# A merging stage that begins with half-products while its attention tiles are still being merged

## The reference, cut to what matters

```python
def merge_by_denominator(outs, lses):
    wts = jax.nn.softmax(jnp.stack(lses, 0), axis=0)
    return jnp.sum(wts[..., None] * jnp.stack(outs, 0), axis=0)
...
    mix = jnp.concatenate([o_dn.reshape(B, S, DN_V), o_at.astype(x.dtype).reshape(B, S, AT_W)], axis=-1) @ w_out
    x = x + rmsnorm(mix, g_post_mix)
```

## Time and profile before

| | us |
|---|---|
| median of 3 runs | 3841.65 |
| lowest, highest | 3839.93, 3842.64 |
| the profiled execution | 3840.81 |
| its span | 3839.0 |
| TensorE busy in the span | 3418.6 (89%) |

### The profile page before, as it was taken

One profiled execution on the slowest core, in us unless ns is written; L12 is line 12 of the kernel. 1 busy time (PEld: TensorE's weight loads), 2 busy tenths in 40 slices (PEclk: granted clock), 3 DMA queues, 4 the chain that ended last, 5 costly groups with the idle time before them and its releaser, 6 DMA issues. The chain is left out here.

```text
span 3839.0 us, 61619 instructions
## 1 busy us (share of the span) xinstructions
PE 3418.6 (89%) x24762; PEld 3234.8 (84%) x24762; DVE 1667.2 (43%) x2263; ACT 1198.5 (31%) x2487; POOL 840.7 (22%) x460
## 2 busy tenths in 40 slices
PE   7999999647888888884979999999999799999697
PEld 6899999426777677774978999999999799999697
DVE  6553122445656666665856122111121333443465
ACT  4111122215655555552325001111100244432332
POOL 3111111011111211124313111111111245554132
PEclk9999999768989999996999999999999899999898
DMA  3223344542333233325342333411111255553321
GB/s 111 73 67 88 111 180 158 184 124 75 92 92 81 69 94 91 89 60 172 121 147 105 127 127 127 146 39 39 39 42 44 97 172 189 202 204 125 121 80 70
DMA packets 278812, 420.05 MB, mean 109 GB/s; under 512 B 65022, under 2 KB 222398, under 8 KB 268432
## 3 DMA queue, kind: packets, MB, share of 16 engines
q1 hardware_dynamic: 278616, 417.30, 34.2%
HBM read 292.65 MB, written 158.13 MB: 117 GB/s over the span
## 5 line engine op out<-in xcount | busy, mean ns | idle before, releaser
L78 PE MATMUL pd_prod<-pd_h_hi,pd_whi 128*128 128x412 f32 x1760 | 616.3, 350 | 25.9 <-DVE pd_h_lo L2420 25.9
L79 PE MATMUL pd_prod<-pd_h_hi,pd_wlo 128*128 128x412 f32 x1760 | 616.3, 350 | 0.0
L80 PE MATMUL pd_prod<-pd_h_lo,pd_whi 128*128 128x412 f32 x1760 | 616.2, 350 | 0.0
L78 PE MATMUL pa_proj<-pa_h_hi,pa_whi 128*128 128x412 f32 x1160 | 407.5, 351 | 32.9 <-DVE pa_h_lo L408 24.2
L79 PE MATMUL pa_proj<-pa_h_hi,pa_wlo 128*128 128x412 f32 x1160 | 407.3, 351 | 0.0
L80 PE MATMUL pa_proj<-pa_h_lo,pa_whi 128*128 128x412 f32 x1160 | 406.0, 350 | 0.0
L78 PEld LDWEIGHTS pd_prod<-pd_h_hi,pd_whi 128*128 128x128 f32 x1760 | 331.3, 188 | 29.2 <-issue 25.6
L79 PEld LDWEIGHTS pd_prod<-pd_h_hi,pd_wlo 128*128 128x128 f32 x1760 | 331.4, 188 | 3.0 <-issue 0.8
L80 PEld LDWEIGHTS pd_prod<-pd_h_lo,pd_whi 128*128 128x128 f32 x1760 | 331.1, 188 | 1.4
L78 PE MATMUL pe_prod<-pe_ahi,pe_whi 128*128 128x412 f32 x880 | 311.4, 354 | 23.3 <-DVE pe_alo L2681 21.8
L2579 POOL TENSOR_TENSOR pe_wlo<-pe_w,pe_whi 128x1408 fp32r<-128x1408 f32 x80 | 264.5, 3317 | 235.5 <-ACT pe_whi L2590 235.5
(11 more groups left out here) (377 smaller groups left out, 6494.7 us busy)
## 6 DMA issues: line engine op xcount, KB each, us to landing
pe_w<-in_w_down SPq DMA_DIRECT2D x80, 704.0 KB, 4.0
scratch_at<-pa_work SPq DMA_DIRECT2D x24, 1024.0 KB, 5.6
pb_qkv<-scratch_at SPq DMA_DIRECT2D x32, 768.0 KB, 5.2
pd_w<-in_w_gate_up SPq DMA_DIRECT2D x44, 512.0 KB, 5.6
out_new_cache_k<-in_cache_k SPq DMA_DIRECT2D x8, 2046.0 KB, 9.8
out_new_cache_v<-in_cache_v SPq DMA_DIRECT2D x8, 2046.0 KB, 15.5
pa_w<-in_w_in SPq DMA_DIRECT2D x29, 512.0 KB, 5.7
scratch_a<-pd_act SPq DMA_DIRECT2D x16, 824.0 KB, 3.8
```

The costliest lines, as they stand in the source:

```text
L78: pe.matmul(out, w_hi, a_hi, start=first, stop=False)
L79: pe.matmul(out, w_lo, a_hi, start=False, stop=False)
L80: return pe.matmul(out, w_hi, a_lo, start=False, stop=last)
```

## The change

- SyncE issues w0, the delta half of block 0 and tile 0 first; the two constants (identity and gain) come behind tile 0, then w1 and the tiles 1, 2, 3.
- GpSimd alternates: `split_w(0)`, `scale(0)`, `split_w(1)`, `scale(1)`, up to `scale(4)`, and then `split_w(5)`, `(6)`, `(7)`. Before it did scale(0) to scale(2) behind split_w(0), and scale(4) behind split_w(7).
- ScalarE splits the delta half right behind w0, and w1 to w4 in turn with the exponents and `take`.
- VectorE makes the low part of the delta half first (`low_heads`), and waits for the constants only ahead of tile 2's merging.
- TensorE no longer turns tiles 0, 1, 2 first. It makes the delta half (k = 0 to 3, 12 matmuls) of products 0, 1, 2, 3 with a turn behind each of the first three, then the attention half of products 0 and 1, the delta half of product 4, and from there on turns and second halves. The products 5, 6, 7 are whole, and the turns of tiles 3, 4, 5 stand ahead of the products 2, 4 and 6 as before.

```diff
@@ sync
-            sp.dma_start(ident[:, :], t["consts"][:, 0:P]).then_inc(const_loaded, 16)
-            sp.dma_start(gain[:, :], t["g_post_mix"]).then_inc(const_loaded, 16)
...
             load_w(0)
-            for i in range(3):
+            load_heads(0)
+            load_u(0)
+            sp.dma_start(ident[:, :], t["consts"][:, 0:P]).then_inc(const_loaded, 16)
+            sp.dma_start(gain[:, :], t["g_post_mix"]).then_inc(const_loaded, 16)
+            load_w(1)
+            for i in range(1, 4):
                 load_u(i)
-            load_heads(0)
-            load_w(1)
-            load_u(3)
@@ gpsimd
-            split_w(0)
-            for i in range(3):
-                scale(i)
-            split_w(1)
-            split_w(2)
-            scale(3)
-            for j in range(3, KD):
+            for j in range(KD):
                 split_w(j)
+                if j < 5:
+                    scale(j)
             for b in range(NMB):
                 for n, i in enumerate(tiles(b + 1)):
-                    if i + 1 < NTILE:
+                    if 5 <= i + 1 < NTILE:
                         scale(i + 1)
@@ scalar
             split_w(0)
+            split_heads(0)
             exponents(0)
+            split_w(1)
             exponents(1)
             take(0)
+            split_w(2)
             exponents(2)
             take(1)
-            split_heads(0)
+            split_w(3)
+            exponents(3)
             take(2)
-            split_w(1)
-            exponents(3)
-            split_w(2)
+            split_w(4)
             exponents(4)
-            for j in range(3, KD):
+            for j in range(5, KD):
                 split_w(j)
@@ tensor
-            def products(b, j):
+            def products(b, j, first=0, last=KD):
...
-                for k in range(KD):
+                for k in range(first, last):
...
-                mm.then_inc(prod_done, 1)
-
-            for i in tiles(0):
-                turn(i)
-            for b in range(NMB):
+                if last == KD:
+                    mm.then_inc(prod_done, 1)
+
+            for j in range(MIX_BANKS - 1):
+                products(0, j, 0, HEADS)
+                if j < 3:
+                    if j == 0:
+                        pe.wait_ge(const_loaded, 32)
+                    turn(j)
+            products(0, 0, HEADS)
+            products(0, 1, HEADS)
+            products(0, MIX_BANKS - 1, 0, HEADS)
+            for j in range(2, KD):
+                if j in (2, 4, 6):
+                    turn(3 + (j - 2) // 2)
+                if j < MIX_BANKS:
+                    products(0, j, HEADS)
+                else:
+                    products(0, j)
+            for b in range(1, NMB):
@@ vector
-            dve.wait_ge(const_loaded, 32)
...
+            low_heads()
             weigh(0)
             merge_and_weigh(0)
             merge_and_weigh(1)
             low(0)
+            dve.wait_ge(const_loaded, 32)
             merge_and_weigh(2)
             low(1)
-            low_heads()
             low(2)
```

More of the change, by code:

```diff
@@ L1999, in _ @@
             pe.wait_ge(consts_set, 2)
-            pe.wait_ge(const_loaded, 32)
             def turn(i):
@@ L2012, in mean @@
                 pe.matmul(mean_ps[:, 0:width(b)], ones_mean[:, :], acc[:, 0:width(b)], start=True, stop=True).then_inc(means_done, 1)
-            def products(b, j):
+            def products(b, j, first=0, last=KD):
                 n = b * KD + j
-                if b == 0:
+                if b == 0 and first == 0:
                     pe.wait_ge(w_lo_done, j + 1)
@@ L2029, in products @@
                                         mix_hi[:, b % 2, k, 0:width(b)], mix_lo[:, b % 2, k, 0:width(b)], k == 0, k == KD - 1)
-                mm.then_inc(prod_done, 1)
-            for i in tiles(0):
-                turn(i)
-            for b in range(NMB):
+                if last == KD:
[17 more added lines that the diff above has]
+            for b in range(1, NMB):
                 following = list(tiles(b + 1))
                 for j in range(KD):
-                    if b and j == 1:
+                    if j == 1:
                         mean(b - 1)
```

## The result

| | before | after |
|---|---|---|
| median of 16 runs each, us | 3841.62 (3837.41 to 3848.31) | 3849.41 (3841.75 to 3857.07) |
| ratio, 95% interval | | 1.0021 (1.0014 to 1.0029) |
| the profiled execution, us | 3840.81 | 3841.75 |
| first DMA of the stage, in that execution | 1753.76 | 1749.83 |
| first DMA of the next stage | 2006.99 | 2009.04 |

The change costs 7.8 us (5.4 to 11.1 by the interval). The forecast was +1.5 us and "no difference". The profiled execution of after is the fastest of its 16, and it entered the stage 3.9 us early for reasons of its own, so the two traces can't be laid on each other by their clocks.

A forecast was written before the change was run, and what follows sets the result against it. TensorE was taken as the bound once going, with tile 5's turn also set by w5's low part, the loads and `low(3)`. Landing and turn 0.0, cold restart +2.2, later waiting -0.7: net +1.5, 3843.2 us, range 3837.5 to 3849.5.

The forecast's parts named there:

- no difference: Whole kernel: the stall moves from tile 4's turn to tile 5's, change under 0.2% (7.7 us); chance 0.81.
- The bound and the new stall: TensorE in block 0: the 13.2 us stall at tile 4's turn goes, one of about 12 us precedes tile 5's.
- The opening: Stage start: TensorE's first half product near 1764, 18 us ahead of 1781.94, with slack against tile 5's turn.
- w5's low part, "one us later": GpSimd's low part of w5: done at 1803.4 against 1802.37, one us later.
- The cycle of 7.4: Tiles 1 to 4, with a GpSimd weight between additions: 2.4 + 5.0 = 7.4 us a tile.
- 0.6 for that: w2's landing in the crowded queue: ready 0.6 us after GpSimd could have used it.
- My sign for the mechanism: VectorE's merging: `L2087` at over 2 us for tiles 1 to 4, with a GpSimd weight in each gap.
- The landing, "-1.0": Block 1's delta half: lands 11.87 - 1.0 us behind w7's issue, at 1814.3, the same as before.
- The cold restart, "+2.2": Tile 5's turn and the matmuls behind it at the lower clock after the new stall: +2.2 us together.
- "Later 2.2 us of waiting can soak up a part: -0.7": A later TensorE wait of 2.2 us ahead of a turn absorbs part of the loss: -0.7 us.
- The chance of 0.13 for slower: Rival, GpSimd's alternation of weights and tiles: each us per tile counts four times before w5; 3849.6 us, chance 0.13.
- a cycle of about 9 us: Tiles 1 to 4: the time per tile above which the slower rival decides, w5's low part then at 1809.8.

The follow-up runs named there:

- e2: The kernel before, with one move: GpSimd scales and adds tile 4 ahead of weight 5 instead of behind weight 7; 3848.17 us, ratio 1.0014.
- e3: The changed kernel, with block 1's delta half loaded right behind w5 instead of behind w7 and x; 3841.98 us, ratio 0.9999.
- e4: The kernel before, with block 1's delta half loaded right behind w5; 3843.91 us, ratio 1.0002.
- e6: The changed kernel, with block 1's delta half loaded behind w5 and other work reordered so that tile 5's turn can come sooner; 3839.70 us, ratio 0.9988.
- e7: The kernel before, with its old opening, tile 4 ahead of weight 5 and the same moves as e6; 3838.72 us, ratio 0.9985.
- e9: The changed kernel unaltered, run again for a second profile; one time, 3844.93 us.
- e5: The changed kernel, with SyncE issuing tile 8 only when block 1's delta half has landed; 3848.29 us, ratio 1.0010.
- e1: The changed kernel with GpSimd's old order alone put back, the other engines keeping the new order; 3852.35 us, ratio 1.0024.
- e10: The changed kernel with 64 filler matmuls on TensorE ahead of tile 5's turn; 3850.79 us, ratio 1.0018.
- e8: e6 with the delta halves of blocks 3 to 5 issued at the start of their round; 3834.41 us, ratio 0.9976.

## Why the prediction was wrong, step by step

- **The bound and the new stall: right.** "The 13.2 us stall is gone and a new one of about 12 us stands ahead of the turn of tile 5": 12.38 us, through the lines foreseen. e2 makes it with one move, e3 takes half of it away and with it the whole loss, e4 shows that the shortened chain wasn't the bound before.
- **The opening: right in kind.** First half product at s 10.0 (10.2 foreseen), and worth nothing (e6 against e7).
- **w5's low part, "one us later": too small, the first step that failed.** +2.1 us in after (s 50.7 against 48.6), +2.4 in e9. Tile 0 was merged 0.4 us earlier than foreseen, the four cycles after it took 1.6 us more. The cycle of 7.4 was right for tiles 3 and 4 (7.3, 7.4) and wrong for tiles 1 and 2 (8.0, 9.0). There the loads were late in the crowded queue: tile 1 by 1.22 us, and w2 so late that GpSimd began its weight 1.63 us after it was free. I had 0.6 for that, and nothing for an operation that slides into the weight because it is late. My sign for the mechanism, `L2087` at over 2 us for tiles 1 to 4, held for tiles 2 and 4 only; at tile 1 another small operation paid in its place.
- **The landing, "-1.0": wrong in sign, the second step that failed.** It is 12.55 us behind w7, not 10.9, and 0.7 longer than before. e5 clears tile 8 of more than 0.3 us. What is left is that an empty queue doesn't pay back. Before, transfers were already running when w7 was issued (256 GB/s in the 2 us after its issue, against 119 after), and that bandwidth wasn't lost time. The other traces with this chain fall in line: e1, with 234 GB/s in those 2 us, took 12.1 us; e2, e5, e9 and e10, with 119 to 182, took 12.6 to 12.9. That the slow start of the queue is the whole 0.7 us was not tested.
- **The cold restart, "+2.2": of the right size.** 1.2 to 2.5 us against e10's warm restart, with the turn's own 0.5 in it.
- **"Later 2.2 us of waiting can soak up a part: -0.7": of either sign.** Everything behind block 0's mean added 0.6 us in after, where that wait grew to 2.85, and took off 1.2 in e9, where it shrank to 1.5.

The sum by these terms: +2.7 for the turn (2.1 + 0.7 - 0.1), +2.7 for the restart with it, +0.6 later: 6.0 us, and that is the stage in the profile (259.2 against 253.2). In e9 it is 3.6: +3.3, +1.5 and -1.2. The forecast was 1.5: 0.0, +2.2 and -0.7. So the mechanism was right, and the steps that failed are two sizes in the sum, w5's low part and the landing, which together were put at 0.0 and were 2.7 to 3.3 us. In after the later waiting adds 1.3 us to the miss and the longer restart 0.5. Together they moved a forecast that lay inside the 0.2% to its edge. The chance of 0.13 for slower was too low. I had priced it by a cycle of about 9 us alone; the four cycles averaged 7.9, and the loss came from several smaller terms together, two of which, the crowded queue and the stopped small operations, could hardly come out better than taken.

What stays open: the median rose by 7.8 us (at least 5.4), the stages of the two profiled executions of the changed kernel by 6.0 and 3.6, so 1.8 to 4.2 us of the 7.8 aren't found in this stage. The rest of a run takes between 1831 and 1837 us behind the stage in these traces, and the stage starts between 1750 and 1761, so single profiles don't settle 2 us.

## What to carry to other kernels

Where a wait is about to be removed, look at the next place at which the same engine meets another, and ask how long ago the other one was ready. A place with no idle time can be two chains ending together, and a list of waits names neither. Then follow what the moved instruction delays, through the queue of loads that is issued in order behind it. And take a load off such a chain by its place in the issue order: moving one DMA (e3) was worth as much as the whole re-ordering had cost, and moving three more (e8) removed a wait of 4.3 us and gave the lowest time relative to the kernel before.

## What the runs showed of the hardware that I had not expected

- VectorE's operations on eight columns are stopped by a GpSimd operation as fully as large ones: 0.17 us became 2.27 (`L2074` at 1766.50), ending with GpSimd's weight at 1768.75. The exclusive lock that "SBUF — State Buffer" (Who interferes with whom) of the Trainium skill states fits each of the rows shown. What the operation pays is what is left of GpSimd's when it starts: 2.27 us at 1766.50, 2.25 at 1776.19, 2.08 at 1791.12, but 0.36 at 1785.42.
- The delta half issued behind w7 and x landed 12.55 us after the issue of w7 with an empty queue and 11.9 with a backlog, while w7 itself took 3.35 and 5.5.
